# Neighbourhood attention in a two-block transformer kernel: the grid row becomes the innermost index of the bias copies in DRAM

## The reference, cut to what matters

```python
dr_i = (row_idx - r[:, None]) + (NA_KR - 1)
dc_i = jnp.clip(c[None, :] - c[:, None], -(NA_KC - 1), NA_KC - 1) + (NA_KC - 1)
bias = rpb.astype(jnp.float32)[:, dr_i[:, None, :, None], dc_i[None, :, None, :]]
bias = jnp.where(in_win[None, None, :, None, :], bias, NEG_INF)
...
s = jnp.einsum('bhrcd,bhrikd->bhrcik', qg, k_blk) * scale + bias[None]
p = jax.nn.softmax(s.reshape(b, NA_HEADS, rows, GRID_W, kr * GRID_W), axis=-1)
```

## Time and profile before

| | |
|---|---|
| median of 3 runs | 2303.08 us (2303.01 to 2303.67) |
| span of the profiled execution, first to last instruction | 2302.1 us |
| what lies around the span, against the median | 1.0 us |
| TensorE busy | 2292.6 us, granted clock 1.00 |
| DVE, ACT, Pool busy | 1494.8, 1316.3, 67.5 us |
| the four copies to `na_skew` are issued | 35.6 to 169.3 us |
| the 32 bias loads are issued | 88.4 to 257.2 us |
| the masked sums run | 175.8 to 298.9 us |

### The profile page before, as it was taken

One profiled execution on the slowest core, in us unless ns is written; L12 is line 12 of the kernel. 1 busy time (PEld: TensorE's weight loads), 2 busy tenths in 40 slices (PEclk: granted clock), 3 DMA queues, 4 the chain that ended last, 5 costly groups with the idle time before them and its releaser, 6 DMA issues.

```text
span 2302.1 us, 32533 instructions
## 1 busy us (share of the span) xinstructions
PE 2292.6 (100%) x11831; PEld 1919.8 (83%) x11831; DVE 1494.8 (65%) x2102; ACT 1316.3 (57%) x1998; POOL 67.5 (3%) x94
## 2 busy tenths in 40 slices
PE   9999999999999999999999999999999999999999
PEld 7887778888888888888888888888887888888887
DVE  5647555556577775467776677787977665555554
ACT  5456564444565554355555577667674566666653
POOL 0011100000100000000000001010000000000000
PEclk9999999999999999999999999999999999999999
DMA  8789997777866666566567856676855797987974
GB/s 269 220 258 255 267 246 219 217 212 220 245 190 193 193 183 201 174 206 195 183 187 204 243 165 193 167 204 179 229 147 175 220 252 228 266 218 233 263 222 167
DMA packets 416529, 489.61 MB, mean 213 GB/s; under 512 B 146160, under 2 KB 242320, under 8 KB 416272
## 3 DMA queue, kind: packets, MB, share of 16 engines
q1 hardware_dynamic: 409984, 479.33, 70.7%
q10 hardware_dynamic: 6416, 8.56, 1.1%
HBM read 429.07 MB, written 35.41 MB: 202 GB/s over the span
## 4 chain that ended last, share of the span: by engine, by line
PE 92%; DVE 3%; ACT 2%; DMA 1%; DVEq 1%; SPq 1%; issue 1%; ACTq 0%
PE gemm L789 22%; PE gemm L790 22%; PE gemm L791 22%; PE gemm L777 7%; PE aux L777 7%; PE gemm L769 4%; PE aux L769 4%; DVE w_lo L733 1%; DMA raw<-in_w_in 1%; ACT w_hi L723 1%; PE aux L789 1%; PE aux L791 1%; PE aux L790 1%; PE aux L2452 0%; PE aux L2860 0%
## 5 line engine op out<-in xcount | busy, mean ns | idle before, releaser
L733 DVE TENSOR_TENSOR w_lo<-raw,w_hi 128x1024 fp32r<-128x1024 f32 (+1 forms) x800 | 954.6, 1204 | 585.2 <-ACT w_hi L723 581.7
L723 ACT ACTIVATE w_hi<-raw 128x1024 fp32r<-128x1024 f32 (+1 forms) x800 | 813.4, 1041 | 470.7 <-PE gemm L791 287.8
L789 PE MATMUL gemm<-w_lo,hT 128*128 128x512 f32 x1600 | 632.8, 396 | 2.2 <-DVE w_lo L733 1.6
L791 PE MATMUL gemm<-w_hi,hT 128*128 128x512 f32 x1600 | 623.4, 390 | 0.0
L790 PE MATMUL gemm<-w_hi,hT 128*128 128x512 f32 x1600 | 623.1, 389 | 0.0
L789 PEld LDWEIGHTS gemm<-w_lo,hT 128*128 128x128 f32 x1600 | 300.5, 188 | 69.7 <-issue 5.2
L791 PEld LDWEIGHTS gemm<-w_hi,hT 128*128 128x128 f32 x1600 | 300.4, 188 | 63.6
L790 PEld LDWEIGHTS gemm<-w_hi,hT 128*128 128x128 f32 x1600 | 300.6, 188 | 59.4 <-issue 0.2
L777 PE MATMUL gemm<-hT,w_hi 128*128 128x512 f32 x704 | 216.6, 392 | 0.0
L777 PE MATMUL aux<-hT,w_hi 128*128 128x512 f32 x672 | 207.6, 390 | 0.0
L789 PE MATMUL gemm<-w_lo,yT_hi 128*128 128x512 f32 x472 | 184.0, 390 | 0.0
(11 more groups left out here) (346 smaller groups left out, 2190.0 us busy)
## 6 DMA issues: line engine op xcount, KB each, us to landing
raw<-in_w_up SPq DMA_DIRECT2D x336, 256.0 KB, 3.0
raw<-in_w_in SPq DMA_DIRECT2D x144, 512.0 KB, 5.1
raw<-in_a_w_in SPq DMA_DIRECT2D x128, 512.0 KB, 4.0
raw<-in_b_w_in SPq DMA_DIRECT2D x128, 512.0 KB, 4.7
raw<-in_w_down SPq DMA_DIRECT2D x76, 512.0 KB, 4.6
raw<-in_w_branch SPq DMA_DIRECT2D x32, 512.0 KB, 5.2
raw<-in_w_out SPq DMA_DIRECT2D x32, 512.0 KB, 4.7
raw<-in_a_w_out SPq DMA_DIRECT2D x32, 512.0 KB, 4.2
```

The costliest lines, as they stand in the source:

```text
L723: nc.scalar.activation(hi, src, ACT.Copy).then_inc(S("hi_done"), 1)
L733: nc.vector.tensor_tensor(lo, src, hi.bitcast(F32), ALU.subtract).then_inc(S("lo_done"), 1)
L789: nc.tensor.matmul(dst, xh, wl[:, k, :], start=h["start"] and k == 0, stop=False)
L791: mm = nc.tensor.matmul(dst, xl, wh[:, k, :], start=False, stop=h["stop"] and k == h["n"] - 1)
```

## The change

The bias in DRAM and in SBUF gets the row difference as its innermost index, 64 columns by 7 row differences in place of 7 by 128.

ACT's queue loads the whole table (16 partitions of 3584 bytes) at the start. After tile 0, ACT waits for it, writes a turned copy in SBUF (`table_turned`, 16 partitions of 896 elements, read with a stride), and waits for that. The four copies to `na_skew`, of the same size and at the same places in the program, now have `table_turned` in SBUF as their source: 4 partitions, each read 64 times. A bias load reads one run of 448 values (1792 bytes) a partition instead of 6 runs of 256 bytes. The bias buffers are 8 tensors of 128 by 64 by 7, and Pool issues one `affine_select` for each head, so 8 of 64 by 336 elements for a pair of heads instead of 4 of 64 by 576. The masked sum of a head becomes two instructions of 128 by 256, one for each token block, and their bias operand steps by 7 values from column to column.

```diff
-        bias = r.put("bias", [P, BR, 2, SPAN, GRID])
+        bias = [[(spare if (b, a) == (0, 0) else r).put(f"bias{b}{a}", [P, GRID, NKR - 1]) for a in range(2)] for b in range(BR)]
+        table = q.put("rpb_rows", [NAH, NKR - 1, P])
+        table_turned = q.put("rpb_columns", [NAH, P, NKR - 1])
...
-                src = bass.AP(tensor=na_skew.tensor, offset=(2 * u + h) * GRID * SKEW + (1 - a) * P + GRID - 1,
-                              ap=[[SKEW - 1, GRID], [P, SPAN], [1, GRID]])
-                sp.dma_start(bias[a * GRID:(a + 1) * GRID, u % BR, h, :, :], src).then_inc(S(f"bias_landed{u % BR}"), 16)
+                src = bass.AP(tensor=na_skew.tensor, offset=(2 * u + h) * GRID * SKEW + (GRID - 1) * (NKR - 1) + 1 - a,
+                              ap=[[SKEW - (NKR - 1), GRID], [1, GRID * (NKR - 1)]])
+                sp.dma_start(bias[u % BR][h][a * GRID:(a + 1) * GRID, :, :].rearrange("p k s -> p (k s)"),
+                             src).then_inc(S(f"bias_landed{u % BR}"), 16)
...
+            act.dma_start(table[:, :, :], ins["na_rpb"][0]).then_inc(S("rpb_rows"), 16)
+
+            def copy_table(h, n):
+
+                src = table_turned[h:h + n, :, :].rearrange("h x s -> h (x s)")
+                src = bass.AP(tensor=src.tensor, offset=src.offset, ap=[list(src.ap[0]), [0, GRID], [1, SKEW]])
+                act.dma_start(na_skew[h:h + n], src).then_inc(S(f"na_copied{h // 4}"), 16)
...
+                if t == 0:
+                    act.wait_ge(S("rpb_rows"), 16)
+                    A(table_turned[:, :, :], table[:, :, :].rearrange("h s x -> h x s"), ACT.Copy).then_inc(S("rpb_rows"), 1)
+                    act.wait_ge(S("rpb_rows"), 16 + 1)
                 if t in (0, 2):
-                    copy_bias(na_skew, ins["na_rpb"], SKEW, f"na_copied{t // 2}", 2 * t, 4)
+                    copy_table(2 * t, 4)
...
-                        V.scalar_tensor_tensor(out=part, in0=score_banks(u % 2)[a][:, :].rearrange("p (t k) -> p t k", t=TB),
-                                               scalar=float(NAD) ** -0.5, in1=window, op0=ALU.mult, op1=ALU.add)
+                        for tb in range(TB):
+                            window = bias[u % BR][a][:, :, 2 - 2 * tb:2 - 2 * tb + T // GRID].rearrange("p k s -> p s k")
+                            V.scalar_tensor_tensor(out=part[:, tb, :].rearrange("p (s k) -> p s k", k=GRID),
+                                                   in0=score_banks(u % 2)[a][:, tb * T:(tb + 1) * T].rearrange("p (s k) -> p s k", k=GRID),
+                                                   scalar=float(NAD) ** -0.5, in1=window, op0=ALU.mult, op1=ALU.add)
```

More of the change, by code:

```diff
@@ L32 @@
 NKR, NKC, GRID = 8, 16, 64
-SPAN = 6
 F = 5504
@@ L224, in program @@
         BR = 4
-        r = Region(scratch - 2 * nbytes([P, 2, SPAN, GRID]))
-        bias = r.put("bias", [P, BR, 2, SPAN, GRID])
+        r = Region(y_at + nbytes([P, 2 * UP1 + KD, T]))
+        spare = Region(y_at + nbytes([P, KD + 4, T]))
+        bias = [[(spare if (b, a) == (0, 0) else r).put(f"bias{b}{a}", [P, GRID, NKR - 1]) for a in range(2)] for b in range(BR)]
         mix_at = r.at
+        q = Region(y_at)
+        table = q.put("rpb_rows", [NAH, NKR - 1, P])
+        table_turned = q.put("rpb_columns", [NAH, P, NKR - 1])
         ga = Region(mix_at).put("ga", [P, TB, D])
@@ L857, in _ @@
                 for a in range(2):
[L858 to L861, removed]
-                    pool.drain()
-                    nc.gpsimd.affine_select(out=above, in_=above, compare_op=ALU.is_ge, fill=NEG, base=NKC // 2 - 1 - NKC,
-                                            pattern=[[0, 2 * SPAN], [-1, GRID - NKC]],
-                                            channel_multiplier=1).then_inc(S("bias_masked"), 1)
+                    both = [bias[u % BR][h][a * GRID:(a + 1) * GRID, :, :] for h in range(2)]
+                    for v in both:
+                        below = v[:, 0:GRID - NKC, :]
+                        nc.gpsimd.affine_select(out=below, in_=below, compare_op=ALU.is_ge, fill=NEG, base=NKC // 2,
+                                                pattern=[[1, GRID - NKC], [0, NKR - 1]], channel_multiplier=-1)
+                    pool.drain()
+                    for v in both:
+                        above = v[:, NKC:GRID, :]
+                        e = nc.gpsimd.affine_select(out=above, in_=above, compare_op=ALU.is_ge, fill=NEG, base=NKC // 2 - 1 - NKC,
+                                                    pattern=[[-1, GRID - NKC], [0, NKR - 1]], channel_multiplier=1)
+                    e.then_inc(S("bias_masked"), 1)
             if parts >= 3:
@@ L1787, in masked @@
                         dve.wait_ge(S("na_scores"), 2 * u + a + 1)
-                        b0 = bias[:, u % BR, a, 2, 0:1]
-                        window = bass.AP(tensor=b0.tensor, offset=b0.offset,
-                                         ap=[list(b0.ap[0]), [-2 * GRID, TB], [1, T]])
                         part, at = sc[u % 2][:, :, a * T:(a + 1) * T], u % 2 * 2 + a
-                        V.scalar_tensor_tensor(out=part, in0=score_banks(u % 2)[a][:, :].rearrange("p (t k) -> p t k", t=TB),
-                                               scalar=float(NAD) ** -0.5, in1=window, op0=ALU.mult, op1=ALU.add)
+                        for tb in range(TB):
[3 more added lines that the diff above has]
+                                                   scalar=float(NAD) ** -0.5, in1=window, op0=ALU.mult, op1=ALU.add)
                         dve.drain()
```

## The result

The changed kernel takes 2419.1 us in the median against 2303.21 us, a ratio of 1.0502 (95% interval 1.0491 to 1.0513): 116 us more. The forecast was 2392 us with a range up to 2420, and 2402 to 2412 with the lower clock. So the time lies 1 us inside the range and above what the clock was given. One execution of 9165.53 us is left out of the ratio but counted in the median; the other five have a median of 2418.36 us.

The account below looks back on a forecast made before the run. The prediction took TensorE's pace to bound the kernel. Its terms, 84 + 1.8 + 4 - 0.7 = +89 us on a span of 2302.1, with the median 1.0 us above the span, gave 2392 us, range 2306 to 2420.

Parts of the forecast that it names:

- The copies' source: Copies to `na_skew` read four SBUF partitions; their rate was bounded between 8.8 us and 35.3 us a copy.
- the high end: Four neighbouring partitions together give only one engine's 26 GB/s, so a copy takes 35.3 us, 26.5 more.
- The stalls: TensorE waits for weights beside each of the four copies: 21 us each, 84 us in all.
- lead: Weights TensorE has in hand at copies that don't stall today: 2.7 us taken off each copy's stall.
- one more half: One more half of the weight stream slips in during a long copy: 2.7 us taken off its stall.
- The price of a half: A half of the weight stream beside a long copy takes 12.6 us; three get through in 35.3 us.
- The clock: Rival: long stalls also lower TensorE's clock, making 2402 to 2412 us; chance 0.1, kept out of the sum.
- (d): The rival of a lower TensorE clock for one or two halves after each copy: 2402 to 2412 us, chance 0.1.
- ACT after tile 0: ACT's turning copy and its wait delay the first copy's issue and the weight halves behind it: +1.8 us.
- Masked sums, masks and loads: Attention side: strided sums of 596 ns on DVE, +4 us; Pool's masks nothing; shorter bias loads -0.7 us.
- Pool's term: Pool's 4 to 8 masks a pair, each below 1.15 us, are done in time and cost nothing.
- main step: The rate of a DMA from four neighbouring SBUF partitions is one engine's; likeliest case, chance 0.68, 2350 to 2420 us.

Follow-up runs that it names:

- e2: The kernel before, with its table in 16 partitions of SBUF, unturned, as the source of the copies: 2399.41 us, ratio 1.042.
- e3: The changed kernel, with the table loaded eight times so that head h lies in partition 8h: 2328.44 us, ratio 1.0111.
- e12: The changed kernel with its table in all 128 partitions; copy j reads partitions j, j+32, j+64 and j+96: 2347.6 us, ratio 1.0192.
- e1: The changed kernel without the SBUF source and ACT's turning copy; the table is laid out turned in DRAM and copied from there: 2320.02 us, ratio 1.0073.
- e4: The kernel before, with the table loaded to SBUF, turned by ACT and waited for, the copies still from DRAM: 2307.34 us, ratio 1.0018.
- e6: e1 with each of Pool's masks cut to one column: 2311.89 us, ratio 1.0039.
- e9: e1 with both a dense bias operand for the masked sums and Pool's masks cut to one column: 2303.82 us, ratio 1.0003.
- e5: e1 with a dense bias operand for the masked sums, which add other values than the bias: 2315.8 us, ratio 1.0056.

## Why the prediction came out as it did

**The copies' source: right.** The forecast took the high end, 35.3 us a copy, because four neighbours should have one engine's worth between them. It is 35.2 to 36.6, and e2, e3 and e12 leave no other cause: the same bytes from SBUF take 12, 18 or 36 us by which partitions they lie in. That the figures meet so closely is in part chance. The 35.3 was for a copy alone; beside the weights the copy's own packets fill 33 us on each of its engines (0.217 x 16 x 38 / 4), and weight packets the rest.

**The stalls: 84 us forecast, 80.8 measured, by two errors that cancel.** It was 21 us each, against 20.8, 20.7, 21.0 and 18.4. The forecast let a copy grow by 26.5 us, from 8.8. But 8.8 is a copy alone; beside the weights it took 12.1 to 13.7 us before, so it grew by 21.5 to 24.4. Of the growth the forecast took off 5.4 us as lead and for one more half; measured, growth less stall is 0.8 to 5.3 us, 3.0 on average. The price of a half was off too: 12.6 us each and three a copy, where the two halves that end the stalls landed 26 and 34 us after their issue. The forecast had nothing for SP, whose issues grow to between 3.6 and 4.3 us, but that cost little, as the issue times above show.

**The clock: a rival of 0.1 that happened.** The sum went without it and (d) gave it 10 to 20 us. TensorE's busy time shows 23.6 us, of which e2 has 17.2 and e1 5.0. Behind each stall of 13 us and more, and behind those of some 5 us and the one of 3.08 as well, matmuls run at the lower level (1.2 GHz), 0.43 us apart instead of 0.22. This is the largest term missing from the 2392.

**ACT after tile 0: 1.8 forecast, 4.5 measured (e4).** The turning copy takes 1.80 us and not 1.0: the nearest row was a dense 1024 elements on 128 partitions, and this one reads 896 with a stride. The stall is 3.08 us. The rest is TensorE busy 1.2 us longer in e4, at the lower clock.

**Masked sums, masks and loads: +3.3 forecast, 17.2 measured (e1).** This is the step of the forecast that failed. The price of the sum was near, 596 forecast and 635 measured, so L2053 was the right row for a strided operand. Wrong was Pool's term, "so nothing". The forecast asked only whether Pool is done in time, and took each mask to be below 1.15 us; they take 1.2 us undisturbed and 1.5 on average, eight in place of four for a pair. And Pool's time is not free for DVE even when nobody waits for a mask; e6 and e9 show it. The kernel before had a hint that I did not read. Its scaling took 394 ns on average:

```profile
L1807 DVE TENSOR_SCALAR scores<-scores,row_inv 128x256 f32<-128x256 f32 x32 | 10.6, 394 | 0.6
```

Once Pool was done, four of them took 1.14 us. The bias loads did become shorter, 480 ns in the median against 586, and gave back nothing (e9).

By idle and busy time the growth of the span is 80.8 (copies) + 23.6 (clock) + 3.1 (ACT) + 7 (what is left, the attention side) = 114.5 us; the forecast had 84 + 0 + 1.8 + 3.3 = 89. The 27 us that the forecast was short are not in its main step: they are the clock, kept out of the sum as a rival, and Pool, priced by whether someone waits for it.

The range held by 1 us, and that is luck. No sum in the forecast leads to its top of 2420, and the clock's own range ended at 2412. Had the stalls come out at 84 us and not 80.8, the time would have been outside.

## What to carry to other kernels

A DMA's rate depends on which partitions it touches as well as on how many. Before a small table in SBUF becomes the source of a large copy, spread its rows over partitions that don't share a path (here 8 apart), or leave it in DRAM. An engine that nobody waits for can still cost time: when work on Pool doubles, price every DVE instruction that runs beside it. And when stalls are forecast (here they were 3 to 16 us long), add the matmuls at the lower clock behind them; here they were about a quarter on top of the idle time (23.6 on 90.9 us).

## What the runs showed of the hardware that was not expected

- A slow copy on four DMA engines holds up the transfers of another queue that are spread over all sixteen. Weight halves landed in up to 34 us, the last of them 0.3 to 0.6 us after the copy's last packet, while the engines were mostly at 2 to 3 tenths. SP's issues grew to 3.6 to 4.3 us each.
- Pool's `affine_select` of 64 by 336 takes 1203 ns with 7 elements inside and 48 outside, 791 ns the other way round, and 734 ns for 64 by 576 with 48 inside (the fastest of each).
- Four `tensor_scalar` of 128 by 256 on DVE took 1.14 us beside an idle Pool and 3.73 us beside a masking one, where three of the four ended 0.15 us after a mask.
- Two causes on the same places of the path gave back 16.4 us together and 4.5 and 8.4 alone. With one of them taken away TensorE still stood idle for 3.2 us at each of its two longest places there (e5), or for 2.8 and 2.4 us (e6).
